# A third feed-forward tile in a bank pair of its own, begun before the second norm's factor is known

## The reference, cut to what matters

```
x = x + rmsnorm(mix, g_post_mix)
u = rmsnorm(x, g_pre_ffn) @ w_up                      # 1024 -> 2 x 2816
uc = conv_b + sum_i u_ext[:, i:i+T] * conv_w[i]       # causal, width 3, per channel
f = (gelu(gate, approximate=True) * val) @ w_down     # gate, val: the halves of uc
x = x + rmsnorm(f, g_post_ffn)
```

## Time and profile before

| | |
|---|---|
| runs | 1933.11, 1934.1, 1937.15 us |
| median | 1934.1 us |
| the profiled execution | 1937.56 us; its span 1935.4 us |
| TensorE matmul busy | 1862.3 us, 96% of the span |
| DVE, ACT, POOL busy | 966.1, 559.3, 994.6 us |
| mean granted TensorE clock | 0.996 of full speed |

### The profile page before, as it was taken

The page is one execution under the profiler, slowest core; times in us unless marked ns, Lnnn a source line. Parts: engine busy times, 40 slices in busy tenths (PEclk is TensorE's granted clock), DMA queues, the critical chain, the costliest instruction groups (busy, mean ns, idle before and its releaser), DMA issues. The chain is left out here.

```text
span 1935.4 us, 34011 instructions
## 1 busy us (share of the span) xinstructions
PE 1862.3 (96%) x14662; PEld 1803.8 (93%) x14662; DVE 966.1 (50%) x1527; ACT 559.3 (29%) x1164; POOL 994.6 (51%) x580
## 2 busy tenths in 40 slices
PE   7989999999999999999998899999999999999999
PEld 6889888999899999999998888889998999999998
DVE  7668566322555541523657766653226555325153
ACT  3334343212422221201344333431124222112021
POOL 5536415455455555556554634145564555555553
PEclk9999999999999999999999999999999999999999
DMA  4222201224122222222242212112241222222222
GB/s 163 90 77 89 77 23 66 77 88 145 66 88 88 88 88 88 89 86 90 99 145 84 93 56 72 39 55 88 88 145 63 90 89 88 88 88 88 79 88 90
DMA packets 74597, 168.40 MB, mean 87 GB/s; under 512 B 6032, under 2 KB 33552, under 8 KB 74448
## 3 DMA queue, kind: packets, MB, share of 16 engines
q1 hardware_dynamic: 67264, 158.84, 24.5%
q10 hardware_dynamic: 7184, 7.38, 1.1%
HBM read 156.41 MB, written 9.79 MB: 86 GB/s over the span
## 5 line engine op out<-in xcount | busy, mean ns | idle before, releaser
L1480 PE MATMUL ps<-xn,wsp 128*128 128x272 f32 x7872 | 1017.2, 290 | 28.9 <-issue 19.5
L1480 PEld LDWEIGHTS ps<-xn,wsp 128*128 128x128 f32 x7872 | 997.6, 190 | 35.5 <-issue 23.4
L570 POOL CAST wsp<-raw 128x1024 fp32r<-128x1024 f32 (+1 forms) x278 | 304.4, 1095 | 803.3 <-DMA raw<-in_wstream 634.0
L572 POOL TENSOR_TENSOR wsp<-raw,wsp 128x1024 fp32r<-128x1024 f32 (+1 forms) x278 | 671.0, 2414 | 22.3
L1480 PE MATMUL ps<-R,wsp 128*128 128x272 f32 x3840 | 486.2, 288 | 0.1
L1480 PEld LDWEIGHTS ps<-R,wsp 128*128 128x128 f32 x3840 | 482.7, 189 | 1.3 <-DVE xT L1063 0.5
L1034 DVE SCALAR_TENSOR_TENSOR R<-ps,R 64x256 fp32r<-64x256 f32 (+8 forms) x232 | 128.3, 560 | 66.6 <-ACT R L698 27.5
L1378 DVE TENSOR_TENSOR mix<-ps,rstd 128x272 f32<-128x272 f32 x88 | 38.9, 442 | 210.8 <-PE ps L1480 200.5
L925 ACT ACTIVATE mix<-vv 128x2 f32<-128x2 f32 x88 | 18.0, 205 | 371.1 <-DVE mix L1380 371.1
L1034 DVE SCALAR_TENSOR_TENSOR R<-mix,R 128x544 fp32r<-128x544 f32 (+1 forms) x82 | 70.0, 854 | 82.9 <-ACT R L944 68.9
L1191 DVE TENSOR_TENSOR_SCAN xT<-xT 128x128 f32<-128x128 f32 (+3 forms) x64 | 82.9, 1335 | 30.4 <-ACT xT L782 30.4
(11 more groups left out here) (219 smaller groups left out, 1532.1 us busy)
## 6 DMA issues: line engine op xcount, KB each, us to landing
raw<-in_wstream SPq DMA_DIRECT2D x234, 512.0 KB, 3.3
raw<-in_wstream SPq DMA_DIRECT2D x48, 128.0 KB, 2.6
raw<-in_wstream SPq DMA_DIRECT2D x16, 384.0 KB, 3.0
raw<-in_kc SPq DMA_DIRECT2D x8, 512.0 KB, 4.0
raw<-in_vc SPq DMA_DIRECT2D x8, 512.0 KB, 4.2
xT<-in_x_in SPq DMA_DIRECT2D x4, 544.0 KB, 6.5
out_k_out<-mix ACTq DMA_DIRECT2D x8, 272.0 KB, 2.6
xT<-in_x_in SPq DMA_DIRECT2D x1, 2176.0 KB, 8.0
```

The costliest lines, as they stand in the source:

```text
L570: nc.gpsimd.tensor_copy(dst[:, 0, 0:w], part).then_inc(S["w_hi"], 1)
L572: nc.gpsimd.tensor_tensor(dst[:, 1, 0:w], part, dst[:, 0, 0:w].bitcast(F32), ALU.subtract).then_inc(S["w_lo"], 1)
L1480: mm = pe.matmul(z[:, h], w[:, x, (k0 + k) * P:(k0 + k + 1) * P], rhs[:, y, k, h * HT:(h + 1) * HT], start=(k == 0 and (x, y) == (0, 0)), ...
```

## The change

`("upg", 1)` gets banks 6 and 7, where the first norm's factor was. TensorE waits before it for `r_mul` to reach 8, that is until DVE has used that factor for the last time. As the first convolution tap of ("upv", 0) goes to the same banks 6 and 7 (`uc[1]`), ScalarE waits before it until DVE has read ("upg", 1), and DVE reads ("upg", 1) right behind ("upv", 0), ahead of the taps of ("upv", 0). No instruction is added or removed apart from waits. The tiles behind take the rotating pairs in turn, now one place shifted: ("upv", 1) takes the pair of ("upg", 0), ("upg", 2) that of ("upv", 0), and from ("upv", 2) on each takes that of the second last tile, as before.

```diff
-        UPPER = {("nm", 1): (6, 7), ("nm", 2): (4, 5), ("nm", 3): (6, 7), ("nm", 0): (6, 7),
+        UPPER = {("nm", 1): (6, 7), ("nm", 2): (4, 5), ("nm", 3): (6, 7), ("nm", 0): (6, 7), ("upg", 1): (6, 7),
                  ("pleg", 2): (4, 5), ("pleg", KT - 1): (4, 5), ("q", 0): (4, 5), ("k", 0): (6, 7)}
...
                         act.wait_ge(S["act_step"], n + 1)
                         if v and j > 0:
                             act.wait_ge(S["g_raw"], j)
+                        elif v:
+                            act.wait_ge(S["dve_read"], dread(("upg", 1)))
                         ac(uc[v], e[:, 0:T + 2], ACT.Identity, scale=vv[:, V_CW + f:V_CW + f + 1],
...
                             for j in range(_F0[part], _F0[part + 1]):
-                                u_tile(("upg", j))
+                                if j != 1:
+                                    u_tile(("upg", j))
                                 if j > _F0[part]:
                                     g_low(part, j - 1)
                                 taps(("upg", j))
                                 u_tile(("upv", j))
+                                if j == 0:
+                                    u_tile(("upg", 1))
                                 taps(("upv", j))
...
                             for t in _up(part)[2 if part == 0 else 0:]:
+                                if t == ("upg", 1):
+                                    pe.wait_ge(S["r_mul"], KT)
                                 project(t, t, xn, KT)
```

## The result

| | before | changed |
|---|---|---|
| median | 1933.86 us (7 runs, 1927.7 to 1937.15) | 1923.58 us (7 runs, 1922.01 to 1926.14) |
| the profiled execution | 1937.56 us, span 1935.4 | 1926.14 us, span 1924.0 |
| mean granted clock there | 0.996 | 0.997 |

The ratio is 0.9946, with a 95% interval of 0.9932 to 0.9961: faster by 0.5%, and by more than was forecast. The means are 1925.6 us over its 30 runs and 1935.0 us over those 104. The first comparison, 10.3 us in the medians, was thus somewhat favourable, and the gain to explain is 9.4 us.

A forecast was written before the change was run, and what follows sets the result against it. TensorE, busy for 96% of the span, was taken to bound the kernel. From the median of 1934.1 us, 4.86 us for the two waits and 0.76 us for the clock came off, giving 1928.5 us, range 1925.0 to 1932.0 us.

The forecast's parts named there:

- What bounds the place: Before ("upg", 1) in both layers: TensorE idles 2.43 us, waiting only for DVE to read ("upg", 0).
- The wait that goes: Before ("upg", 1): with banks 6 and 7 TensorE starts 2.43 us earlier in each layer, 4.86 us in all.
- Does TensorE stand later instead?: At ("upv", 1), ("upg", 2), ("upv", 2): no new wait; the tightest, ("upv", 2), has 2.8 us of cover; cost nothing.
- The port: DVE's low part beside POOL's subtraction: held until 536.9, about 1.0 us by the skill page, at most 2.2; cost nothing.
- rival 3: DVE late before ("upv", 2): two stretches of 2.2 us make TensorE wait 1.6 us a layer; 1931.7 us, chance 0.04.
- The clock: Behind the two gaps: one clock fall cost 1.52 us; half of it, 0.76 us, counted as saved, bounds 0 and 3.04.
- Rival 1: Clock falls follow both gaps as a rule, or the shift removes one in the attention; 1926.2 or 1924.7 us, chance 0.10.
- I count them at zero: Clock falls in both layers' attention: the 2.4 us shift may remove or add some, about 1.5 us each; counted as nothing.
- The sum: Whole kernel: 1934.1 less 4.86 and 0.76 gives 1928.5 us against the median; 1931.2 us against the profiled execution.
- Rival 2: Only the bare gaps are won; the shift brings one or two falls in the second attention; 1930.8 or 1932.3 us, chance 0.20.
- rival 4: Before ("upg", 1): the remaining `dve_read` wait still includes ("upg", 0), so the gap stays; 1934.1 us, chance 0.04.
- rival 5: Reordered DVE reads only move the wait to ("upv", 2); TensorE stands 6.0 us a layer; slower, 1940.5 us, chance 0.02.

The follow-up runs named there:

- wait_both: Changed kernel with TensorE's wait for DVE's read of ("upg", 0) put back before ("upg", 1) in both layers; 1934.50 us, ratio 0.9994 to the kernel before.
- gap_filled: Changed kernel with the old wait back in both layers, filled with 18 matmuls whose result is overwritten; 1932.13 and 1932.83 us, ratios 0.9990 and 0.9991 to before.

## Why the prediction was right and wrong

- **What bounds the place.** Right. The wait for ("upg", 0) was all that held TensorE, and its weight, `r_mul` and banks were ready in time. The undo shows it: in `wait_both` the wait alone brings the time back.
- **The wait that goes: 2 x 2.43 = 4.86 us.** The mechanism was right, the term 0.74 us short. I took the idle column; start to start it is 2.80 us, 5.6 in all.
- **Does TensorE stand later instead?** Right: no wait before ("upv", 2). The cover was worked out as 2.8 us without, and 0.6 with the longest low part, and measured 2.0. The low part took 2.04 us and not 0.73, as the bound had it. DVE read ("upg", 1) 6.05 us behind the last sum's end (6.3 forecast), and the table load came 0.9 us later than before, counted from there (1.3 forecast).
- **The port.** The low part began at 536.80, inside POOL's subtraction (535.85 to 538.25), and ended at 538.84, 0.59 us behind it; its median alone is 0.73 us. By the page SBUF — State Buffer of the Trainium skill, section Who interferes with whom, which the prediction cites, it is held until that subtraction ends, and this trace agrees. It cost nothing here since the cover held. (For rival 3 the prediction gives 0.79 us to taps and products alike; that is the taps, a product takes 0.69.)
- **The clock: 0.76 us of a possible 3.04.** The first step that failed, in its size and not in its mechanism. I halved the one fall seen, because the three runs then known lay below the profiled execution. In fact half clock followed 7 of 10 gaps, 0.7 x 2 x 1.5 = 2.1 us, and gap_filled agrees. Rival 1 named this case, 1926.2 or 1924.7 us, and got 0.10; the mean over 30 runs is 1925.6.
- **"I count them at zero": half clock in the attention.** The second failure, and a larger one. A shift was taken to bring as much as it takes. The second attention of the changed kernel meets 0.6 stretches and not 1.8, some 2 us. I had also counted one stretch there, at 1256 us, where the same trace of before has two:

```profile
1129.00:1133.00 4.00, 3.73 (x19) 0.59 0.00 0
```

- **The sum** is then 5.6 + 2.1 + 2 = 9.7, against 9.4 measured over all runs and 5.6 forecast. The first two terms are shown by the undone wait and the filled gap. That the third belongs to the change, through the moment of the second attention, is likely and not proven, and its cause is open.
- **Luck.** The seven runs of the first comparison lost 4.7 us to half clock, the 23 later ones 7.1. Without that draw the time of 1923.58 us would have been about 1926, just inside the stated range of 1925.0 to 1932.0, with the same steps failed.
- **Rival 2** gave 0.20 to the wrong direction of that same shift. Rivals 3, 4 and 5 did not come.

## What to carry to other kernels

Price a gap of TensorE from start to start, and add the half clock that may follow it. One trace does not tell the second term (one gap in two had it in each trace of the kernel before, 7 in 10 overall); take several before halving it. A bank whose last reader is early can take the next tile whose normal bank waits for a late one, if the consumer that writes that bank later has slack, and that slack should be worked out at the first tile behind where readers were reordered.

## What the runs showed of the hardware

- Idle time of 2.43 us was followed by half clock in 7 of 10 cases, at about 1.5 us each; idle time of 3.77 and 3.73 us in both of two. The same 2.43 us filled with matmuls of no use were followed by full clock in all 4 places of two traces. The Trainium skill's page TensorE: Matmul & The Clock Gate (Part 1: The HAM clock gate) says that the monitor runs free of the kernel; the run-to-run spread, 1927 to 1948 us for one and the same kernel, agrees: with each run's loss to half clock taken off, its standard deviation falls from 3.3 to 1.3 us.
- Where the work lies in time may matter on average too: 2.6 us more loss to half clock (2.2 against the runs beside them) in kernels that differ from the changed one by nothing but 1.4 or 2.9 us of busy matmuls. A monitor of random phase alone would not give that, and it was not explained.
- A pair of DVE scans took 4.66 us or 3.14 us in two traces of kernels with the same attention; the cause was not tested.
